# Attention phase: low parts of the output weights moved to GpSimd, and four places in the order of work changed

## The reference

```python
h = x @ w_in                                    # q, k, v of 8 MoBA heads and 8 FoX heads, and 8 forget logits
# MoBA (256 tokens are one block): causal softmax(q k / 8 + relative bias) v
# FoX: causal softmax(q k / 8 + c_t - c_s) v, with c = cumsum(log_sigmoid(f + b_f))
m = concat(o_moba, o_fox) @ w_out               # 1024 x 1024
x = layer_norm(ALPHA * x + m, g, b)
x = layer_norm(ALPHA * x + 0.5 * swiglu(x, w_gate, w_up, w_down), g, b)
```

## Time and profile before

| what | value |
|---|---|
| time, median of 3 runs | 1019.13 us (1018.92 to 1019.48) |
| the profiled execution: its own time | 1019.3 us |
| its span, first to last instruction | 1017.6 us |
| TensorE busy | 1007.7 us (99%) |
| VectorE, ScalarE, GpSimd busy | 617.0, 448.6, 41.9 us |

### The profile page before, as it was taken

How to read it: one execution, slowest core, us unless ns; L and a number is a source line. 1 busy time by engine, 2 the same in 40 slices (tenths; PEclk the granted TensorE clock), 3 DMA queues, 4 the chain that set the end, 5 groups by cost and what they waited for, 6 DMA issues and landing times.

```text
span 1017.6 us, 12772 instructions
## 1 busy us (share of the span) xinstructions
PE 1007.7 (99%) x4800; PEld 827.6 (81%) x4800; DVE 617.0 (61%) x758; ACT 448.6 (44%) x523; POOL 41.9 (4%) x55
## 2 busy tenths in 40 slices
PE   9999999999999999999999999999999999999998
PEld 7888888888777888888888888888888888888887
DVE  5555455677688745454677544545787864545574
ACT  5444344356563643434356343434344553434441
POOL 0400000100000000000010000000210100000010
PEclk9999999999999999999999999999999999999999
DMA  8875656355227666464449656554467676565531
GB/s 293 262 246 176 207 171 211 112 185 175 85 91 241 222 233 207 165 206 165 165 130 324 208 166 206 167 206 162 140 196 233 206 251 206 168 206 170 196 124 42
DMA packets 129684, 191.47 MB, mean 188 GB/s; under 512 B 5448, under 2 KB 95816, under 8 KB 129520
## 3 DMA queue, kind: packets, MB, share of 16 engines
q1 hardware_dynamic: 126432, 180.11, 53.7%
q0 software_dynamic: 2928, 10.61, 3.1%
q10 hardware_dynamic: 288, 0.26, 0.1%
HBM read 189.90 MB, written 1.06 MB: 188 GB/s over the span
## 4 chain that ended last, share of the span: by engine, by line
PE 92%; DVE 3%; DMA 2%; issue 1%; SPq 1%; ACT 1%; POOL 0%
PE gu L403 20%; PE gu L405 20%; PE gu L404 19%; PE acc L403 9%; PE acc L405 9%; PE acc L404 9%; PE tp L498 4%; DVE g_lo L1152 1%; DMA bias_tab<-in_ffn_w_up 1%; ACT g_hi L867 1%; DMA rawB<-in_sgu_w_out 1%; PE acc L689 1%; DMA rawB<-in_attn_w_out 1%; DMA ws_tok<-in_sgu_w_s 0%; SPq L341 0%
## 5 line engine op out<-in xcount | busy, mean ns | idle before, releaser
L403 PE MATMUL gu<-g_hi,xT_hi 128*128 128x512 f32 x912 | 357.0, 391 | 0.7 <-issue 0.7
L405 PE MATMUL gu<-g_hi,xT_lo 128*128 128x512 f32 x912 | 354.7, 389 | 0.0
L404 PE MATMUL gu<-g_lo,xT_hi 128*128 128x512 f32 x912 | 354.1, 388 | 0.0
L403 PEld LDWEIGHTS gu<-g_hi,xT_hi 128*128 128x128 f32 x912 | 171.3, 188 | 36.2 <-issue 1.7
L405 PEld LDWEIGHTS gu<-g_hi,xT_lo 128*128 128x128 f32 x912 | 171.2, 188 | 35.6
L404 PEld LDWEIGHTS gu<-g_lo,xT_hi 128*128 128x128 f32 x912 | 171.4, 188 | 34.2
L933 ACT ACTIVATE stage<-gu 128x256 f32<-128x256 f32 x88 | 33.7, 382 | 359.3 <-PE gu L405 359.2
L1152 DVE TENSOR_TENSOR g_lo<-rawA,g_hi 128x2048 fp32r<-128x2048 f32 (+2 forms) x66 | 141.4, 2145 | 79.4 <-ACT g_hi L867 79.4
L1278 DVE SCALAR_TENSOR_TENSOR stage<-stage,gu 128x256 f32<-128x256 f32 x88 | 37.0, 420 | 188.0 <-ACT stage L933 188.0
L1152 DVE TENSOR_TENSOR g_lo<-rawB,g_hi 128x2048 fp32r<-128x2048 f32 (+1 forms) x64 | 140.9, 2202 | 16.0 <-ACT g_hi L867 16.0
L403 PE MATMUL acc<-d_hi,hT_hi 128*128 128x512 f32 x352 | 144.8, 411 | 0.0
(11 more groups left out here) (184 smaller groups left out, 682.0 us busy)
## 6 DMA issues: line engine op xcount, KB each, us to landing
rawD<-in_ffn_w_down SPq DMA_DIRECT2D x44, 1024.0 KB, 4.9
rawA<-in_ffn_w_gate SPq DMA_DIRECT2D x42, 512.0 KB, 4.0
rawA<-in_ffn_w_up SPq DMA_DIRECT2D x42, 512.0 KB, 5.0
rawB<-in_ffn_w_gate SPq DMA_DIRECT2D x42, 512.0 KB, 4.4
rawB<-in_ffn_w_up SPq DMA_DIRECT2D x42, 512.0 KB, 5.5
rawA<-in_attn_w_in SPq DMA_DIRECT2D x12, 512.0 KB, 4.3
rawB<-in_attn_w_in SPq DMA_DIRECT2D x12, 512.0 KB, 5.1
rawA<-in_ple_w_gate SPq DMA_DIRECT2D x8, 512.0 KB, 4.8
```

The source lines that it names most:

```text
L403: pe.matmul(dst, hi[b], w_hi[b], start=first and b == 0, stop=False)
L404: pe.matmul(dst, hi[b], w_lo[b], start=False, stop=False)
L405: done = pe.matmul(dst, lo[b], w_hi[b], start=False, stop=last and b == len(hi) - 1)
```

## The change

Four edits. (1) The entries `w_low` leave the list; GpSimd makes the four low parts, with waits on the same high parts and the same signals, after it has issued the loads of the second norm. (2) `inverse 4` stands ahead of `outputs 0 1` and `causal 5`, and `exps 4` too; `inverse 5` stands ahead of `causal 6`; `exps 7` and `inverse 7` stand ahead of `outputs 1 0`. (3) `probs 8` and `probs 9` (the fifth pair) stand behind `g back 5 1`. (4) After attention, x's low part of half 0 stands ahead of the low part of set g0+9's second half.

```diff
-    ("values", 3), ("scores", 4), ("outputs", 0, 1), ("exps", 4), ("causal", 5), ("inverse", 4),
-    ("g front", 5, 1), ("probs", 8), ("probs", 9), ("g back", 5, 1), ("scores", 5), ("exps", 5), ("causal", 6),
-    ("proj", 0), ("p_copy", 0), ("inverse", 5), ("w_out", 0), ("values", 4), ("w_low", 0), ("proj", 1), ("w_out", 1),
+    ("values", 3), ("scores", 4), ("exps", 4), ("inverse", 4), ("outputs", 0, 1), ("causal", 5),
+    ("g front", 5, 1), ("g back", 5, 1), ("probs", 8), ("probs", 9), ("scores", 5), ("exps", 5),
+    ("proj", 0), ("p_copy", 0), ("inverse", 5), ("causal", 6), ("w_out", 0), ("values", 4), ("proj", 1), ("w_out", 1),
     ("p_copy", 1), ("probs", 10), ("probs", 11), ("w_out", 2), ("scores", 6), ("exps", 6), ("proj", 2), ("p_copy", 2),
-    ("inverse", 6), ("causal", 7), ("w_out", 3), ("values", 5), ("w_low", 1), ("proj", 3), ("p_copy", 3),
-    ("probs", 12), ("probs", 13), ("scores", 7), ("outputs", 1, 0), ("exps", 7), ("inverse", 7), ("w_low", 2), ("values", 6),
-    ("w_low", 3), ("out piece", 0, 0, 4), ("probs", 14), ("probs", 15), ("w_next", 0), ("w_next", 1),
+    ("inverse", 6), ("causal", 7), ("w_out", 3), ("values", 5), ("proj", 3), ("p_copy", 3),
+    ("probs", 12), ("probs", 13), ("scores", 7), ("exps", 7), ("inverse", 7), ("outputs", 1, 0), ("values", 6),
+    ("out piece", 0, 0, 4), ("probs", 14), ("probs", 15), ("w_next", 0), ("w_next", 1),
...
                     residual(1, 0, r0, (g_done, 2 * out0 + 3))
-                    if kind == "attn":
-                        lo_g(out0 + 2, 1)
                     xT_low(0, end)
-                    if kind == "sgu":
-                        lo_g(out0 + 2, 1)
+                    lo_g(out0 + 2, 1)
...
+                if ln == 0:
+
+                    n = bases[1]["g"] + 7
+                    for part in range(2):
+                        for rows in range(2):
+                            if rows == 0:
+                                pool.wait_ge(out_high_front, part + 1)
+                            else:
+                                pool.wait_ge((high_a, high_b)[part], n)
+                            ks = slice(4 * part + 2 * rows, 4 * part + 2 * rows + 2)
+                            done = pool.tensor_tensor(g_lo[:, n % 2, ks, :], (rawA, rawB)[part][:, 2 * rows:2 * rows + 2, :],
+                                                      g_hi[:, n % 2, ks, :].bitcast(F32), ALU.subtract)
+                        done.then_inc((split_a, split_b)[part], 1)
```

More of the change, by code:

```diff
@@ L1502, in _ @@
                             low(lo, src, hi).then_inc(tok_ready, 1)
[L1503 to L1514, removed]
                     lo_g(g0 + 8, 1)
```

## The result

The changed kernel takes 1021.38 us (median of 13 runs, 1020.58 to 1021.64), the kernel before 1019.1 us beside it: a ratio of 1.0023 with a 95% interval of 1.0016 to 1.0030. It is 2.3 us slower where 3.7 us faster was forecast, and it lies outside the range. The last rival, with 7% and a price of 1021.5, is what happened.

What follows compares the result with a forecast made beforehand. TensorE, busy 99% of the span, was taken as the bound, so only gaps in its starts could be won. 1.7 + 0.6 + 1.0 - 0.1 + 0.9 - 0.4 = 3.7 us, giving 1015.5 us, range 1014.5 to 1016.9.

Steps and rivals of the forecast that it cites:

- The last rival: GpSimd's pieces hold VectorE's mask rows 6, inverse 6 and mask rows 7; some 6 us reach TensorE, 1021.5 us; 7%.
- one input at one element a cycle did not: Argument against holds: only a subtraction of two SBUF operands held the other engine, a one-input VectorE operation did not.
- the rule against this change: Skill's rule that fast VectorE modes and GpSimd lock each other out; set aside because mask rows seemed one element a cycle.
- GpSimd delays nobody: Claim for low parts on GpSimd: its next duty is the norm behind them, and its loads are issued before.
- part 3: Moving four low parts to GpSimd: pieces of 2.4 us end at 297.0, removing TensorE's 1.02 us wait for rawB.
- rows 7 and 8: Trace rows of GpSimd operations and the VectorE operations beside them, used to price pieces and possible holds.
- Fifth pair's turn and scaling: In attention, set 5's product back moves ahead of the fifth pair's turn, so scores 5 start 1.7 us earlier.
- mask rows behind inverse 5: Takes 1.00 us of mask rows from in front of the sixth pair's scaling; gain 0.6 us on TensorE.
- The doubled one-input row: Price of a GpSimd piece: its 128x1024 one-input time, 1.09 us, taken twice, giving 2.2 to 2.7; 2.4 chosen.
- The wait for rawB: TensorE's 1.02 us wait for a low part ahead of the second block's second half, expected to vanish.
- The next load holds the turn of x: Next phase's weights load moves only 2.3 us earlier, so x's turn keeps its wait; total gain there 3.2 us.
- x's low part first: At the next phase, swapping low parts removes TensorE's 0.9 us wait; 0.35 returns at a later turn, 0.5 net.

Runs made afterwards that it cites:

- order-alone run: The changed kernel with the four low parts back on VectorE, keeping the new order; 1017.84 us, ratio 0.9992 to the kernel before.
- accumulator run of the mask rows: The changed kernel with only the mask rows of pairs 6 and 7 in the accumulator form of tensor_scalar; 1018.9 us, ratio 1.0000 to the kernel before.
- half-piece run: The changed kernel with GpSimd's low parts in eight pieces of 128x512 instead of four of 128x1024; 1019.45 us, ratio 1.0009 to the kernel before.

## Why the prediction was wrong

**The step that failed** is "Against: ... one input at one element a cycle did not", under the rule against this change and in the last rival, and with it "GpSimd delays nobody" in part 3. I divided 768 elements by 1.00 us and called it one a cycle. That takes the fixed cost of four instructions for nothing. Nor did any row show the case: in rows 7 and 8 only GpSimd is seen waiting, never VectorE, and the VectorE instruction beside which GpSimd ran undisturbed (750.04) is no one-input instruction but one with two inputs, one of them in PSUM. So the hold had a price of nothing in the sum, without evidence. The rows by shape, in the kernel before, would have said it (busy us, mean ns, idle):

```profile
L1460 DVE CUSTOM_DVE_ANT_0 logits<-acc,causal_c 128x256 f32<-128x256 f32 x8 | 3.4, 423 | 2.1 <-PE acc L689 1.1 <-issue 1.0
...
L1474 DVE TENSOR_SCALAR causal_c<-causal,small 128x256 f32<-128x256 f32 x8 | 2.8, 346 | 0.0
...
L1460 DVE CUSTOM_DVE_ANT_0 logits<-acc,causal_c 128x128 f32<-128x128 f32 x8 | 2.3, 286 | 0.0
...
L1474 DVE TENSOR_SCALAR causal_c<-causal,small 128x128 f32<-128x128 f32 x8 | 2.2, 280 | 0.0
```

The score instruction, which reads PSUM, takes 137 ns more for 128 more elements: one each 1.07 ns. The mask row takes 66 ns more for the same: two at a time. The rest, some 0.2 us, is fixed. So the trace agreed with the Trainium skill (VectorE: DVE Perf Modes, "The perf-mode tier table") where I wrote that it spoke against it. The accumulator form takes 132 ns more for 128 elements, and was not held. The rule of the Trainium skill on who shares a port with GpSimd (SBUF — State Buffer, "Who interferes with whom") excepts this very form, and both runs bear it out. The Trainium skill's condition on size for the mode (Vector Engine (DVE) Microarchitecture Reference, "Performance modes — why throughput varies by op and dtype") is an even count, or an odd one that is the same for source and destination. Two elements meet it, and the 128x2 negation was held 2.15 us.

**Point by point.**
- Fifth pair's turn and scaling, 1.7, and mask rows behind inverse 5, 0.6: 2.3 forecast, 2.4 measured at scores 6 in the changed kernel.
- A piece on GpSimd: 2.4 us forecast, 2.36 to 2.45 measured. The doubled one-input row was a good price. With nobody held, SyncE's issue of rawB came at 296.66 in the accumulator kernel, where 297 was forecast.
- The wait for rawB, 1.0: gone, in the changed kernel and in the accumulator kernel (the changed kernel with every meeting instruction in the accumulator form).
- The next load holds the turn of x, "3.2 in all": the turn came at 316.88 in the accumulator kernel against 320.68, 3.8 earlier. Here I was 0.6 too low: VectorE's residual started at 312.99, 3.8 before, and the turn followed its matmul without a wait. The load of the next weights was issued at 303.47 in place of 306.06, 2.6 earlier where I had 2.3, and ScalarE, waiting for it, could start 5.2 us behind the issue in place of 5.9. VectorE then made the low part at once (310.64), where before it had first finished another residual and its moments (0.8 late). This is most of the excess of 4.1 over 3.7.
- x's low part first, 0.5: measured 0.55, with the return of 0.35 at the turn (0.27 idle ahead of it).
- GpSimd holds nobody: false, -7 us. Scores 6 to the output product takes 14.83 us in the changed kernel (287.91 to 302.74) and 7.84 in the accumulator kernel (287.99 to 295.83). Of the 7.0, 3.7 is the wait at the projection and about 0.8 the one ahead of the seventh pair's turn. The matmuls at the lower clock cost 2.8: 0.5 in six of the projection (2.0 us for 1.5), 0.7 in the turn (1.50 for 0.76), 0.8 in the scores (1.89 for 1.05) and 0.7 in the values (1.48 for 0.8). The accumulator kernel has 0.3 of its own ahead of the output product.

The sum nearly closes: 4.1 gained in the accumulator kernel, less 7.0 for the holds, gives 2.9 slower, against 2.3 measured. Of the 0.6 between them 0.4 lies far behind: at one product of the second mixer TensorE waits 0.74 us for a low part in the accumulator kernel (778.80) and 0.34 in the changed one (785.45). The other 0.2 is as much as the kernel before differed between the two sessions (1019.1 and 1018.86). The rival's price of 6 was made of holds alone, one each on mask rows 6, inverse 6 and mask rows 7 (1.7 + 2.4 + 2.4). In fact three holds, 6.4 us, fell on mask rows 6, none on inverse 6, and one of 2.1 on mask rows 7 that TensorE never waited for. TensorE saw 4.5 us of waits, and the clock, which the rival did not have, made up the rest. The rival's mechanism was right; that its time came within 0.2 us was luck.

Why not a slower order: the order-alone run is not slower than the kernel before (0.9983 to 1.0001). Why not GpSimd's speed: the same pieces cost nothing once the forms differ.

## What to carry to other kernels

Before work goes to GpSimd, list what VectorE runs beside it and take each instruction's cost per element from two shapes, not from a total over a count: in these runs a single-source float32 tensor_scalar in SBUF, the kind that moves two elements at a time, was held to the end of every GpSimd subtraction that was running when it came, even with two elements a partition. Other VectorE instructions beside the pieces were not: the accumulator form, a copy or a score instruction that reads PSUM, a reciprocal. No run has a VectorE instruction with two sources in SBUF beside one of GpSimd's subtractions. Either keep such instructions out of the way (the accumulator form, or a source in PSUM), or give GpSimd short pieces. A gap on TensorE of a few us has to be priced with the slower clock that may come behind it: here it came after waits of 3.7, 2.5 and 2.3 us, and in one profiled execution with a wait of 2.5 it did not.

## What the runs showed that I had not expected

- A 128x2 instruction of 0.17 us held for 2.15 us behind a GpSimd subtraction of 2.36.
- The accumulator form of tensor_scalar costs 0.13 us more at 128x256 (0.474 against 0.346) and is not held: 1.4 us for four mask rows beside a piece, against 7.4.
- VectorE and GpSimd alternate: when GpSimd goes from one piece straight to the next, exactly one waiting VectorE instruction ends, the next starts and is held for the next piece (289.5 and 291.9 us in the changed kernel).
- After 3.7 us of idle TensorE the granted clock was 0.52 from 297 to 303 us and 1.00 from 303 on. A wait of 2.5 us went either way: in the accumulator run of the mask rows the clock fell to 0.50 behind it. In the half-piece run it stayed at 1.00 in the profiled execution, with waits of 2.5, 1.5 and 0.4, but nine of that kernel's eleven executions show a mean of 0.996 to 0.998, and the three at 0.996 took 1020.9 to 1021.1 us.
- GpSimd's tensor_scalar with a pointer scalar takes 0.59 to 1.04 us for 128 or 256 columns, more than its affine select of 256 columns on one operand (0.40) would suggest.
